# The first gate's accumulator summed by adding transfers in place of TensorE

## The reference

```python
mod = silu(c) @ w_ada + b_ada                      # 2048 -> 6 x 2048
sh_m, sc_m, gt_m, sh_f, sc_f, gt_f = split(mod, 6) # each one row of 2048
h = rms_norm(x, g_pre_mix) * (1 + sc_m) + sh_m
proj = h @ w_in                                    # attention heads, GLU and convolution
mix = concat([y_attn, y_conv]) @ w_out
x = x + gt_m * rms_norm(mix, g_post_mix)           # gt_m: the first gate
h = rms_norm(x, g_pre_ffn) * (1 + sc_f) + sh_f
x = x + gt_f * rms_norm(peer(h), g_post_ffn)       # 16384 experts, top 16 per head
```

## Time and profile before

| | us |
|---|---|
| median of 3 runs | 1759.13 (1758.56 to 1760.4) |
| the profiled execution | 1760.12 |
| its span, first to last instruction | 1758.1 |
| TensorE (PE) busy | 1732.3 |
| VectorE (DVE) busy | 1535.3 |
| ScalarE (ACT) busy | 799.5 |
| GpSimd (POOL) busy | 603.1 |

### The profile page before, as it was taken

One profiled execution on the slowest core, in us unless ns is written; L12 is line 12 of the kernel. 1 busy time (PEld: TensorE's weight loads), 2 busy tenths in 40 slices (PEclk: granted clock), 3 DMA queues, 4 the chain that ended last, 5 costly groups with the idle time before them and its releaser, 6 DMA issues.

```text
span 1758.1 us, 28277 instructions
## 1 busy us (share of the span) xinstructions
PE 1732.3 (99%) x9480; PEld 1517.9 (86%) x9480; DVE 1535.3 (87%) x2469; ACT 799.5 (45%) x1185; POOL 603.1 (34%) x413
## 2 busy tenths in 40 slices
PE   7999999999999999999999999999999999999998
PEld 5888888644999999999999999988888888888886
DVE  4668899967688898998999999989999999999997
ACT  3001222300545555556555555554455544555454
POOL 1000000011000388788688888613321211112110
PEclk9999999999999999999999999999999999999999
DMA  9999986699798777987899999999999999999994
GB/s 380 421 421 422 424 322 252 234 387 417 301 349 272 219 218 223 296 253 224 249 382 389 399 411 404 401 365 411 414 413 410 390 404 398 397 399 389 407 387 190
DMA packets 142648, 617.22 MB, mean 351 GB/s; under 512 B 45347, under 2 KB 45939, under 8 KB 87411
## 3 DMA queue, kind: packets, MB, share of 16 engines
q1 hardware_dynamic: 80530, 410.04, 60.0%
q0 software_dynamic: 55712, 202.52, 31.9%
q10 hardware_dynamic: 6336, 3.75, 0.7%
HBM read 598.19 MB, written 16.89 MB: 350 GB/s over the span
## 4 chain that ended last, share of the span: by engine, by line
PE 76%; DMA 9%; DVE 8%; POOL 4%; issue 2%; ACT 1%; DVEq 0%; ACTq 0%; POOLq 0%; SPq 0%
PE ps L1448 33%; PE ps L1110 14%; PE ps L1117 9%; DMA raw<-in_w_ada 7%; PE ps L1161 5%; PE ps L1331 5%; POOL weights L570 3%; PE ps L1172 2%; DVE raw L1547 2%; PE ps L1103 2%; PE ps L1277 2%; DMA early<-in_w_front 1%; DVE w_low L1489 1%; DVE big L1603 1%; POOL big L555 1%
## 5 line engine op out<-in xcount | busy, mean ns | idle before, releaser
L805 ACT ACTIVATE w_hi<-raw 128x1024 fp32r<-128x1024 f32 x444 | 468.8, 1059 | 458.6 <-PE ps L1448 187.4
L1489 DVE TENSOR_TENSOR w_low<-raw,w_hi 128x1024 fp32r<-128x1024 f32 x444 | 541.5, 1224 | 85.5 <-ACT w_hi L805 77.6
L570 POOL DMA_INDIRECT weights<-sel x192 | 366.0, 1906 | 69.2 <-issue 57.6
L1110 PE MATMUL ps<-a,w_hi 128*128 128x384 f32 x1920 | 383.9, 341 | 0.8 <-issue 0.8
L1110 PEld LDWEIGHTS ps<-a,w_hi 128*128 128x128 f32 x1920 | 326.9, 189 | 1.6 <-issue 1.0
L1448 PE MATMUL ps<-w_low,a 128*128 128x512 f32 x1024 | 273.8, 389 | 0.0
L1448 PE MATMUL ps<-w_hi,a 128*128 128x512 f32 x1056 | 268.1, 389 | 1.5 <-ACT big L918 1.5
L1117 PEld LDWEIGHTS ps<-a,w_low 128*128 128x128 f32 x1920 | 247.1, 191 | 2.6 <-DVE w_low L1489 2.3
L1117 PE MATMUL ps<-a,w_low 128*128 128x192 f32 x1920 | 248.2, 271 | 0.7 <-DVE w_low L1489 0.6
L1448 PEld LDWEIGHTS ps<-w_hi,a 128*128 128x128 f32 x1056 | 198.2, 188 | 42.6 <-ACT big L918 1.6
L1448 PEld LDWEIGHTS ps<-w_low,a 128*128 128x128 f32 x1024 | 192.3, 188 | 39.8
(11 more groups left out here) (240 smaller groups left out, 2008.2 us busy)
## 6 DMA issues: line engine op xcount, KB each, us to landing
raw<-in_peer_u SPq DMA_DIRECT2D x128, 1024.0 KB
raw<-in_peer_v SPq DMA_DIRECT2D x256, 512.0 KB
early<-in_w_front SPq DMA_DIRECT2D x56, 1024.0 KB, 11.4
raw<-in_w_ada POOLq DMA_DIRECT2D x48, 1024.0 KB, 9.6
raw<-in_w_ada SPq DMA_DIRECT2D x32, 1024.0 KB
raw<-in_peer_wq SPq DMA_DIRECT2D x16, 1024.0 KB
big<-in_w_gate_f POOLq DMA_DIRECT2D x16, 1024.0 KB, 6.0
weights<-third SPq DMA_DIRECT2D x16, 768.0 KB, 19.1
```

Of the source, the lines that this page charges most:

```text
L570: gp.indirect_dma_start(weight_elements, bass.IndirectOffsetOnAxis(ap=put_at[:, c:c + 1], axis=0), put_gate[:, c:c + 1], None, compute_op= ...
L805: act.activation(high_at(ph, j), raw[:, s % RING, :], ACT.Copy).then_inc(hi_ready, 1)
L1110: done = pe.matmul(ps[:, b % 2, 0:2 * TD].rearrange("p (m t) -> p m t", m=2), high_at(ph, j)[:, k * P:(k + 1) * P], a_pair[:, kc, :, 0:TD] ...
L1489: dve.tensor_tensor(w_low[:, s % RING, :], raw[:, s % RING, :], high_at(ph, j).bitcast(F32), ALU.subtract).then_inc(lo_ready, 1)
```

## The change

TensorE no longer sums the first gate. POOL folds `acc_gate` by seven adding transfers, issued between the `w_ada` blocks 55 to 58: folds 0 and 1 behind block 55, 2 and 3 behind block 56, 4 and 5 behind block 57, fold 6 behind block 58, each after the one before has landed. ACT, after the last head's `put_y`, sends the sum's row to DRAM (`mix_gate_saved`), reads it back as 128 x 16, waits for VectorE's one small product with g_post_mix (`mix_g`, now loaded as 128 x 16 too), writes the product to DRAM and broadcasts it into `gate_row`. VectorE takes up the small product after column sum 17 and goes on with 18 to 22 before it needs the row. `mix_g` and `mix_gate` are two rows of `modc` that are free by then; `g_row` is gone.

```diff
+FOLDS_BEHIND = ((0, 1), (2, 3), (4, 5), (6,))
 # POOL
             for n in range(A_GATE, N_A):
                 gp.wait_ge(mod_used, max(A_GATE, n - SLOTS + 1))
                 gp.dma_start(mod_slots[n % SLOTS], w_ada[n]).then_inc(mod_in[n % SLOTS], 16)
+                if 0 <= n - SLOTS + 1 - MOD_GATES < len(FOLDS_BEHIND):
+                    for fold in FOLDS_BEHIND[n - SLOTS + 1 - MOD_GATES]:
+                        if fold:
+                            gp.wait_ge(gate_sum_ready, 16 * fold)
+                        span = FOLDS[fold]
+                        gp.dma_start(acc_gate[0:span, :], acc_gate[span:2 * span, :], accum_op=ALU.add)\
+                            .then_inc(gate_sum_ready, 16)
 # ACT
-            act.dma_start(g_row, rows[2, :].partition_broadcast(P)).then_inc(g_row_in, 16)
+            act.wait_ge(h_made_first, KC)
+            act.dma_start(mix_g, rows[2, :].rearrange("(p a) -> p a", p=P)).then_inc(g_row_in, 16)
...
             put_y(PAIRS - 1)
-            act.wait_ge(gate_made, 4)
             act.dma_start(gate_g[:, :], rows[3, :].rearrange("(p a) -> p a", p=P)).then_inc(g_row_in, 16)
+            act.wait_ge(gate_sum_ready, 16 * len(FOLDS))
+            act.dma_start(mix_gate_saved, acc_gate[0:1, :]).then_inc(gate_moved, 16)
+            act.wait_ge(gate_moved, 16)
+            act.dma_start(mix_gate, mix_gate_saved[0, :].rearrange("(p a) -> p a", p=P)).then_inc(gate_moved, 16)
+            act.wait_ge(gate_made, 1)
+            act.dma_start(mix_gate_saved[0, :].rearrange("(p a) -> p a", p=P), mix_gate).then_inc(gate_moved, 16)
+            act.wait_ge(gate_moved, 48)
+            act.dma_start(gate_row, mix_gate_saved[0, :].partition_broadcast(P)).then_inc(gate_moved, 16)
 # TensorE
             mix_step(0, 6)
-            pe.wait_ge(mod_used, MOD_GATES)
             pe.wait_ge(ln_var, 1)
             pe.wait_ge(y_ready, PAIRS)
-            for g in range(4):
-                done = pe.matmul(ps[:, MIX_SECOND[g], :], ones[:, :], acc_gate[:, g * 512:(g + 1) * 512],
-                                 start=True, stop=True)
-            done.then_inc(gate_sum_ready, 1)
             mix_step(0, 7)
-            pe.wait_ge(gate_made, 4)
 # VectorE
-            column_sums(10, 15)
-            dve.wait_ge(gate_sum_ready, 1)
-            dve.wait_ge(g_row_in, 16)
-            for g in range(4):
-                cols = slice(g * 512, (g + 1) * 512)
-                dve.tensor_tensor(gate_row[:, cols], ps[:, MIX_SECOND[g], :], g_row[:, cols], ALU.mult)\
-                    .then_inc(gate_made, 1)
-            column_sums(15, 22)
-            dve.wait_ge(gate_made, 4)
+            column_sums(10, 18)
+            dve.wait_ge(gate_moved, 32)
+            dve.wait_ge(g_row_in, 32)
+            dve.tensor_tensor(mix_gate, mix_gate, mix_g, ALU.mult).then_inc(gate_made, 1)
+            column_sums(18, 23)
+            dve.wait_ge(gate_moved, 64)
...
-            column_sums(22, 2 * KC - 1)
+            column_sums(23, 2 * KC - 1)
```

More of the change, by code:

```diff
@@ L192, in build_block @@
         gate_row = region(25984, D)
-        g_row = region(28032, D)
         keysT = region(30080, 2, KEYS)
@@ L282, in build_block @@
         gate_cols = macc[:, 0, :]
+        mix_g, mix_gate = modc[:, 0, :], modc[:, 1, :]
         lam_sum, lam_exp, neg_lam = tiny[:, 0:2], tiny[:, 2:4], tiny[:, 4:5]
@@ L289, in build_block @@
         x_saved = nc.dram_tensor("x_saved", (P, 2 * D), F32, kind="Internal").ap()
+        mix_gate_saved = nc.dram_tensor("mix_gate_saved", (1, D), F32, kind="Internal").ap()
         gate_saved = nc.dram_tensor("gate_saved", (1, D), F32, kind="Internal").ap()
@@ L324, in build_block @@
             sem("ln_n"), sem("z_ready"))
-        gate_sum_ready, gate_made = sem("gate_sum_ready"), sem("gate_made")
+        gate_sum_ready, gate_made, gate_moved = sem("gate_sum_ready"), sem("gate_made"), sem("gate_moved")
         mix_first = sem("mix_first")
```

## The result

Six runs of the changed kernel took 1767.89 us (median; 1767.6 to 1768.86), six of the kernel before in the same comparison 1759.07 us: a ratio of 1.005, 95% interval 1.0039 to 1.0061. The medians differ by 8.8 us. The profiled execution took 1767.74 us, 7.6 more than that of before, which itself lies 1.0 us above the median of its kernel: differences read from the two profiles are smaller than those of the medians by about that much, and where in the span that microsecond lies is not known. The forecast was 1762.4 us with 1766.5 as its upper end, so it was too low; the sign and the mechanism are those of rival 2, at a price above the one given there.

A forecast was written before the change was run, and what follows sets the result against it. In this stage TensorE waits for T, which the full DMA engines set. T +1.55 (-2.25 + 2.50 + 0.3 + 1.0), less 0.2 at the front, plus 1.9 slow restart made +3.25: 1762.4 us, range 1756.5 to 1766.5.

The forecast's parts named there:

- rival 2: Folds hold up POOL 5.1 us each, block 59 leaves at 361: fold cost 4.3 us, 1763.8 to 1765.7 us; chance 0.24.
- the term of the seven folds: POOL's chain of folds makes w_ada blocks 58 and 59 leave late, at about 353 and 357: 1.0 us on T.
- T: End of column sum 30 on VectorE, 435.31 us before the change, which TensorE waits for; forecast to move by +1.55 us.
- The hole: DMA engines underused from 384 to 392 during VectorE's 6.2 us wait for TensorE's gate sum; closing it gives -2.25 us.
- The broadcast: Gate row's broadcast from DRAM at about 393 us, in a stretch with full DMA engines: 1.05 MB cost 2.50 us.
- rival 4: VectorE waits anew for the gate row, 6.8 us after column 22: about 1.5 us above the forecast, 1764 us; chance 0.08.
- The small transfers: The sum's row to DRAM, its read back and the product's store on ACT's queue: 0.3 us on T.
- the front: At 141 us, g_row's broadcast leaves ACT's queue, sparing TensorE's one wait for a w_front block there: 0.2 us gained.
- TensorE's eight records: Gate-sum matmuls taken off TensorE, 3.45 us: worth nothing with T unmoved, as they only lengthen its pause before 443.34.
- TensorE's pause: Idle time before x2's transposes, from 1.25 to 6.25 us, followed by a slow restart at the lower clock costing 1.9 us.
- rival 1: TensorE's clock stays high after its pause, so only T's +1.35 counts: 1760.5 us; chance 0.23.
- Rival 3: w_ada blocks wait for the four slots, not bytes: 6.2 us come back, at most 4.6 through TensorE, 1754.5 us; chance 0.11.

The follow-up runs named there:

- no_folds: Changed kernel without the seven folds, the gate taken from row 0 of the accumulator: 1760.77 us, ratio 1.0006 to the kernel before.
- spread_late: Changed kernel with folds spread behind more w_ada blocks, small product behind column 23, gate_mix behind column 28: 1763.12 us, ratio 1.0021.
- before_later: Kernel before with VectorE's four gate products behind column 16 in place of 14: 1758.14 us, ratio 0.9999.
- early_row: Changed kernel with g_post_mix broadcast early from the input in place of the late broadcast, gate left out of the result: 1765.5 us, ratio 1.0031.
- kept_busy: Changed kernel with 90 unused 128 x 128 products on TensorE ahead of its wait for x2's diagonal: 1775.0 us, ratio 1.0091.
- before_no_sum: Kernel before with the gate's sum, and the wait for it, left out altogether: 1757.15 us, ratio 0.9993.
- folds_ahead: Changed kernel with each fold that stood behind a w_ada block put ahead of it in POOL's program: 1770.48 us, ratio 1.0059.
- run 10: Not a label: "had run 10 us" is TensorE's working time, in the changed kernel with 45 unused products ahead of x2's transposes, 1767.65 us.

## Why the prediction was wrong

**The step that failed is the term of the seven folds:** "With 4.2 and 5 for a block ahead, fold 3 lands at 346, fold 4 at 352, so block 58 is issued at about 353 in place of 350.34 and block 59 at about 357 in place of 352.55 ... I take 1.0, from the median row." It was 8.3 us of T (changed kernel against no_folds). Rows and runs show three things in it that were too small or missing:
- The landings. Fold 3 landed at 351.0, fold 4 at 358.8. Those behind a block took 10.4, 7.8, 7.4 and 6.3 us, the others 4.8, 4.4 and 3.1. From the first issue to the last it is 39.5 us, 6.6 each; the later gate's folds, from which I took the median of one landing, have 5.1 each. That row, not the median, was the one that counts for a chain, and rival 2, which used it, was still short by 2 us at block 59.
- The bytes lost while the blocks were late. I had 0.4 MB; the rows from 350 to 384 show 1.9 MB, 4.5 us at 420 GB/s.
- The blocks ahead of 58. POOL's waits made block 56 leave 1.4 us late (334.06 against 332.62) and block 57 4.0 us late (347.20 against 343.17), which the term left out. From 322 to 350 the engines moved no more than before (229 and 233 GB/s) although some 0.98 MB of it were folds, so about 1.1 MB of the blocks, 2.6 us at 420 GB/s, were left for later. It was not a lack of room: with three of the same folds in this stretch and the blocks on time, spread_late moved 268 GB/s there at a share of 0.86. The room of 9.8 us that the prediction counted was there.

Blocks 56 and 57 in the kernel before (POOL's timeline):

```profile
332.62 0.53 POOL L535 DMA_DIRECT2D raw<-in_w_ada  x1 [9.18 <-DVE macc L1547]
343.17 0.53 POOL L535 DMA_DIRECT2D raw<-in_w_ada  x1 [10.02 <-DVE macc L1547]
```

The Trainium skill, "DMA: Bandwidth & Descriptors", section "Anatomy of one DMA — SWDGE (gpsimd) path", would have had the seven folds done in an estimated 16.4 us; the 39.5 us measured here say that its fixed part is no price for a chain of adding transfers behind other traffic.

**The other steps held in kind, and together they came out 1.7 us better than forecast.** The hole closed (281 to 422 GB/s, by bytes 2.7 us for the 2.25 forecast; in the kernel before its cause is worth 3.0 us of T, by before_later). The broadcast costs 2.5 us (early_row: 2.58). VectorE waits neither for the product nor for gate_mix, so rival 4 is out. The small transfers can't be seen beside the rest: without the folds, hole, broadcast and small transfers give -1.4 us on T (no_folds), forecast +0.35 with the front (-2.25 + 2.50 + 0.3 - 0.2). The front gave 0.56 (block 55 leaves at 322.35), not 0.2, and the hole more than its 2.25; what is left of the 1.7 us is not accounted for. These errors hid part of the folds' price. And the 3.45 us of TensorE's eight records were worth nothing, as argued: TensorE finished mix 4.0 us earlier and waited those 4.0 us longer for T.

**TensorE's pause** was forecast at 6.25 us and is 12.16: 1.25 + 3.45 + 0.54 (front) + 6.92 (x2's delay). It does come back slow, so rival 1 is out; the price is 1.15 us (8.07 - 6.92; 1.2 by kept_busy), not 1.9: the 8 and 64 records run back to back, and the wait for ScalarE between them, 0.46 us in the kernel before and in kept_busy, is gone. The Trainium skill, "TensorE: Matmul & The Clock Gate", section "Part 1: The HAM clock gate", says that an idle array loses its higher clock; the 0.50 from 442 on agrees.

**Sum, as measured:** T +6.92, restart +1.15, given back later -0.3, so the span +7.8 (and the medians +8.8) where +3.25 was forecast. With 8.3 in place of 1.0 for the folds the forecast's own terms give T +8.65, above the 6.92 by what the other terms gained.

Rival 3 (slots, not bytes) is out in the form given: even with no sum and no wait for it (before_no_sum) T comes only 3.2 us earlier, of the 6.2 that this rival gives back (4.6 as far as TensorE lets them). It is partly true of the kernel before: without the 6.2 us wait T comes 3.0 us earlier (before_later), somewhat more than the 2.25 us of the hole.

## What to carry to other kernels

Transfers that depend on each other cost the engine that issues them the sum of their landings, small ones too, and what stands behind them in its program can leave no sooner than their waits let it: before a chain goes into a queue, list what is behind it and when that is due. For a chain take the row of a whole chain (first issue to last), not the median of one landing. Free room in the DMA engines does not help such a chain: here the room was there, and the waits between the steps cost. Work taken from a busy engine ahead of its own pause is worth nothing until what ends that pause comes earlier.

## What the runs showed of the hardware

- An adding transfer from SBUF to SBUF loads the DMA engines beyond its bytes. From 322 to 350 the share rose by 0.20 (5.6 us of the engines) in the changed kernel at about the same GB/s, of which some 0.98 MB were folds; with on-time blocks (spread_late) the share is 0.86 at 268 GB/s, 0.65 at 234 without folds, 5.9 us for 0.95 MB, where 420 GB/s would take 2.3.
- Size explains little of a fold's landing: behind a block's issue the folds of 512, 128, 32 and 8 KB took 10.4, 7.8, 7.4 and 6.3 us to land, the others, of 256, 64 and 16 KB, 4.8, 4.4 and 3.1. That the block in front is the reason isn't shown: taking it away from there did not shorten the chain (folds_ahead, 32.7 us of waiting against 32.9).
- The granted clock fell after a pause of 2.52 us (0.65 from 452 to 453 and 0.50 from 453, while TensorE was back from 450.79; before the pause it had run 10 us at full pace), and after 3.79, 4.36, 7.48, 7.55, 9.30 and 12.16 us; after 1.25 and 1.41 us (before_no_sum) it stayed at 1.00. From x2's transposes to the next ones it is 9.0 to 9.1 us where it stayed, and 9.6 (spread_late) to 10.6 us (no_folds) where it fell. Here the column shows the fall, while in the earlier trace rows it read 1.00 beside records of twice the time.
